# Four buffers for the second one-hots of the gate stage, made by VectorE and ScalarE in turn

## The chip, the cores and the metric

One Trainium2 chip, one core of it. The metric is the device time of one launch in microseconds (us), the median of three runs. PE is TensorE (PEld its weight loads), DVE VectorE, ACT ScalarE, POOL GpSimd, SP SyncE.

## What is computed

The kernel is a two-layer encoder over 256 positions of width 1024. The part of a layer that matters here is PEER, a retrieval of single-neuron experts with product keys:

```python
t1, i1 = lax.top_k(s1, PEER_TOPK)          # 16 of 128 first keys, per head
t2, i2 = lax.top_k(s2, PEER_TOPK)          # 16 of 128 second keys
top_s, top_c = lax.top_k(cand, PEER_TOPK)  # 16 of their 256 sums
experts = e1 * PEER_KEYS + e2
gates = jax.nn.softmax(top_s, axis=-1)
...
act = jax.nn.gelu(jnp.einsum('td,ted->te', h_c, expert_u[e_c]))
out = jnp.einsum('te,ted->td', g_c * act, expert_v[e_c])
```

A position has 8 heads with 16 experts each, so 128 (e1, e2) pairs with a gate each.

## The kernel before

The kernel doesn't gather experts. It runs all 16384 of them in 128 chunks ("up": h times a chunk of expert_u, then gelu; "down": the gated result times the chunk of expert_v) and weights them with a dense matrix `gates` that lives in the tile `arena`. The gate stage, between the up chunks and the down chunks of each layer, turns the 128 pairs of every position into that matrix. For one position it is a 128x128 product: the first one-hots (128 slots by 128 keys, each row scaled by its gate) with the second one-hots. Four positions (HOT = 4) make a batch, and there are 64 batches (N_BATCH) in a layer, written out without a loop. Batch t goes through these steps:

- DVE `hot_firsts`, on even batches only: the first one-hots of two batches at once, a comparison of 128x1024 into `v_raw` (four buffers, reused every four batches; with t the even batch of the pair, it waits until batch t-3 has been multiplied).
- POOL: one multiplication of 128x512 a batch, which scales the first one-hots by the gates (`s_gated`).
- `hot_second`: the second one-hots of the batch, 128x512, in one of three buffers. The first two are the tiles `w_hl` and DVE makes them in one comparison (t % 3 is 0 or 1). The third is the tile `act_w` and ACT makes it (t % 3 is 2) with four Square activations of 128x128 into `apart` (line 1214), a drain and one Relu of 128x512 (line 1216), all at once. Both wait until batch t-3 has been multiplied.
- PE: four fp32 matmuls of 128x128 (line 913; eight in the trace, as each takes two passes), into one of three PSUM banks. They wait for the copy of batch t-3 (`s_gates`), for `s_gated` and for `s_hot2`.
- DVE `gate_early`: the product of the bank and the first 48 chunks' gelu, 128x192, in place in `arena`.
- ACT: a copy of the other 80 chunks' columns, 128x320 (line 1228), after `gate_early` of the same batch.

Every engine takes its own work in the written order. DVE's order at step t is `hot_firsts(t+2)` if t is even, `hot_second(t+2)` if it is DVE's, `gate_early(t)`. ACT's is `hot_second(t+3)` if t % 3 is 2, then the copy of t. PE has five up chunks written in, after batches 7, 17, 27, 37 and 47 (`up_ahead`, line 811, 24 matmuls each). The high parts of the operands of four up chunks are made by ACT at t = 1, 5, 13 and 23 (`high_ahead`, line 1124) and their low parts by DVE after `gate_early` of t = 2, 6, 14 and 24 (`low_ahead`, a subtraction of 128x1024). DVE and POOL call most of their operations in helpers, so DVE's have line 1310 and POOL's line 1800; they are told apart by tile and shape: `v_raw<-ps,side` 128x1024 is `hot_firsts`, `w_hl<-ps,side` is DVE's `hot_second`, `arena<-arena,ps` 128x192 is `gate_early`, `u_hl` or `v_hl<-u_raw` 128x1024 is `low_ahead`, and on POOL `v_raw<-v_raw,side` is the scaling.

After batch 63 the down chunks begin: ACT's `high_v` and DVE's `low_v` of chunk 0 stand behind the stage's last copy.

Of the kernel before, what the change touches and what calls it, by code (L numbers as in the profile page):

```python
# [19 lines left out]
F32 = mybir.dt.float32  # L20
# [6 lines left out]
P = 128  # L27
D = 1024
S = 256
# [10 lines left out]
PK = 128  # L40
# [16 lines left out]
HOT = 4  # L57
# [16 lines left out]
def encoder(nc, x, w_in, w_out, w_glu, w_query, keys, expert_u, expert_v, rel_bias, gains,  # L74
            norm_final, ssm_par, ssm_b, ssm_c, consts, bucket_rows, out):
    ctx = ExitStack()
    with ctx:
# [3 lines left out]
        def sem(name):  # L81
# [30 lines left out]
        hot1_pair = [v_raw[i].rearrange("p (j n) -> p j n", j=2 * HOT) for i in range(2)]  # L112
        hot2 = [rows.rearrange("p r t -> p (r t)").rearrange("p (j n) -> p j n", j=HOT)
                for rows in (w_hl[0][:, :, :], w_hl[1][:, :, :], act_w[:, :, :])]
        early_hl = [u_hl[0][:, :, :, :], u_hl[1][:, :, :, :]] + [
            v_hl[i][:, :, :].rearrange("p r (k n) -> p r k n", k=DC) for i in range(2)]
        iota_ps_cols = slice(S, S + PK)
# [438 lines left out]
        def _(pe):  # L556
# [20 lines left out]
            with pe.Fori(0, DEPTH) as l:  # L577
# [325 lines left out]
                for t in range(N_BATCH):  # L903
                    b, batch = t % BATCHES, l * N_BATCH + t

                    pe.wait_ge(s_gates, batch + 2)
                    pe.wait_ge(s_gated, batch + 1)
                    if t % 3 < 2:
                        pe.wait_ge(s_hot2[0], l * (N_BATCH - N_BATCH // 3) + t // 3 * 2 + t % 3 + 1)
                    else:  # L910
                        pe.wait_ge(s_hot2[1], l * (N_BATCH // 3) + t // 3 + 1)
                    for j in range(HOT):
                        m = pe.matmul(ps[:, t % GATE_BANKS, j * P:(j + 1) * P], hot2[t % 3][:, j, :].bitcast(F32),  # L913
                                      hot1[b][:, j, :], start=True, stop=True)
                    m.then_inc(s_hot_free, 1)
                    if t % GAP_AHEAD == GAP_AHEAD - 3 and ahead < AHEAD:

                        if ahead == 4:
                            pe.wait_ge(s_gelu, 2 + l * PK + EARLY)
                        up_ahead(EARLY + ahead, ahead, early_hl[ahead % 4])  # L920
                        ahead += 1
# [28 lines left out]
        def _(act):  # L950
# [39 lines left out]
            with act.Fori(0, DEPTH) as l:  # L990
# [213 lines left out]
                act.activation(sel_T[:, 2, :], ps[:, 3, 0:S], ACT.Copy).then_inc(s_selT, 1)  # L1204

                split = {1: 4, 5: 5, 13: 6, 23: 7}
                def hot_second(t):

                    act.wait_ge(s_hot_free, l * N_BATCH + t + 2)
                    if t > 2:  # L1210
                        act.wait_ge(s_hot2[1], l * (N_BATCH // 3) + t // 3)
                    for j in range(HOT):
                        o = t * HOT + j
                        act.activation(apart[:, j, :], iota, ACT.Square, scale=-1.0, bias=sel_T[:, 1, o:o + 1])
                    act.drain()
                    act.activation(hot2[t % 3], apart[:, :, :], ACT.Relu, scale=-1.0, bias=one_c)\
                        .then_inc(s_hot2[1], 1)

                act.drain()
                hot_second(2)  # L1220
                for t in range(N_BATCH):
                    if t % 3 == 2 and t + 3 < N_BATCH:
                        hot_second(t + 3)
                    if t in split:
                        high_ahead(split[t])

# [60 lines left out]
        def _(dve):  # L1287
# [21 lines left out]
            def tt(o, a, b, op):  # L1309
                return dve.tensor_tensor(o, a, b, op)  # L1310
# [96 lines left out]
            with dve.Fori(0, DEPTH) as l:  # L1407
# [257 lines left out]

                def hot_second(t):

                    if t % 3 < 2:
                        dve.wait_ge(s_hot_free, l * N_BATCH + t + 2)
                        tt(hot2[t % 3], ps[:, 3, iota_ps_cols].unsqueeze(1).broadcast_to([P, HOT, PK]),  # L1670
                           sel_T[:, 1, t * HOT:(t + 1) * HOT].unsqueeze(2).broadcast_to([P, HOT, PK]),
                           ALU.is_equal).then_inc(s_hot2[0], 1)

# [284 lines left out]
```

## Time and profile before

| | |
|---|---|
| median of three runs | 2128.16 us (2127.49 to 2131.69) |
| the profiled execution's own time | 2125.18 us |
| its span, first to last instruction | 2123.4 us |
| gate stage, each of the two layers | 99.8 us (397.6 to 497.4 and 1445.4 to 1545.2) |
| PE, DVE, ACT, POOL busy over the span | 95%, 76%, 47%, 33% |
| mean granted TensorE clock | 0.988 of 2.4 GHz |

The profile is one execution; the time that is compared is the median. Busy shares of the whole span mix stages with different limits, so the gate stage is read by itself. An instruction's duration in a row includes its latency; two that follow each other at once on an engine start closer together than that, so the pitch (from start to start) is what an engine pays.

### The profile page before, as it was taken

The numbers are of one execution on the slowest core, as the hardware profiler recorded it, in microseconds if no ns is written. First come the engines' busy times: TensorE is split into PE (matmuls) and PEld (weight loads), VectorE is DVE, ScalarE is ACT, GpSimd is POOL, SyncE is SP. The second block draws the span as 40 slices with busy tenths as digits, with TensorE's granted clock in tenths as the row PEclk, the third lists the DMA queues.
The fourth block names the chain that finished last, engine by engine and source line by source line (L and its number), as shares of the span: only waits on it lengthen the run. The fifth ranks groups of instructions, "written<-read, shape, count | busy, mean of one in ns | idle before, by whom it ended". The sixth has DMA issues, their size and how long they took to land.

```text
span 2123.4 us, 37109 instructions
## 1 busy us (share of the span) xinstructions
PE 2022.9 (95%) x11526; PEld 1679.6 (79%) x11526; DVE 1605.3 (76%) x3087; ACT 989.7 (47%) x1627; POOL 695.9 (33%) x537
## 2 busy tenths in 40 slices
PE   7998999988999999999989999998899999999997
PEld 5764999887887888888867559998778788888886
DVE  6993676887779977777779738778867788777775
ACT  3543454664345444444444435546643544444443
POOL 6992566762000400000059816666600013000000
PEclk9999999999999999999999999999999999999999
DMA  5223454203558555555423235542055665555553
GB/s 195 90 71 144 171 183 160 86 21 119 192 198 292 182 196 187 188 188 187 139 91 102 98 134 189 165 146 71 11 170 195 205 219 182 188 188 190 187 192 112
DMA packets 90971, 330.41 MB, mean 156 GB/s; under 512 B 10452, under 2 KB 14676, under 8 KB 88573
## 3 DMA queue, kind: packets, MB, share of 16 engines
q1 hardware_dynamic: 90860, 329.23, 45.8%
q8 instruction: 48, 0.79, 0.1%
q14 instruction: 47, 0.38, 0.1%
q10 hardware_dynamic: 16, 0.02, 0.0%
HBM read 326.04 MB, written 3.16 MB: 155 GB/s over the span
## 4 chain that ended last, share of the span: by engine, by line
PE 78%; issue 7%; DVE 6%; POOL 4%; DVEq 2%; DMA 1%; ACT 1%; ACTq 0%; SPq 0%; POOLq 0%
PE ps L848 31%; PE ps L811 14%; PE ps L821 12%; PE ps L825 5%; PE ps L609 3%; POOL v_raw L1800 3%; PE ps L858 3%; PE ps L775 3%; DVE arena L1310 2%; PE ps L644 2%; PE ps L626 1%; PE ps L604 1%; DVE arena L1480 1%; DVEq L1730 1%; PE ps L727 1%
## 5 line engine op out<-in xcount | busy, mean ns | idle before, releaser
L848 PE MATMUL ps<-v_hl,w_hl 128*128 128x512 f32 x3072 | 734.2, 393 | 15.4 <-DVE v_hl L1310 15.3
L848 PEld LDWEIGHTS ps<-v_hl,w_hl 128*128 128x128 f32 x3072 | 577.4, 189 | 143.8 <-DVE v_hl L1310 22.5
L821 PE MATMUL ps<-h_hl,u_hl 128*128 128x512 f32 x1152 | 418.3, 397 | 0.0
L1800 POOL TENSOR_TENSOR arena<-arena 128x256 f32<-128x256 f32 (+1 forms) x225 | 213.8, 987 | 371.4 <-DVE arena L1310 368.6
L1310 DVE TENSOR_TENSOR v_hl<-v_raw,v_hl 128x1024 fp32r<-128x1024 f32 x208 | 258.6, 1243 | 49.3 <-ACT v_hl L1143 49.2
L825 PE MATMUL ps<-h_hl,u_hl 128*128 128x256 f32 x1008 | 282.6, 280 | 0.0
L1310 DVE TENSOR_TENSOR u_hl<-u_raw,u_hl 128x1024 fp32r<-128x1024 f32 x148 | 186.6, 1261 | 116.0 <-ACT u_hl L1105 113.7
L1143 ACT ACTIVATE v_hl<-v_raw 128x1024 fp32r<-128x1024 f32 x208 | 218.8, 1053 | 113.4 <-PE ps L848 98.9
L821 PEld LDWEIGHTS ps<-h_hl,u_hl 128*128 128x128 f32 x1152 | 216.4, 188 | 45.1
L1105 ACT ACTIVATE u_hl<-u_raw 128x1024 fp32r<-128x1024 f32 x144 | 152.3, 1058 | 135.3 <-PE ps L821 135.3
L1245 ACT ACTIVATE act_w<-act_w 128x256 f32<-128x256 f32 x144 | 60.2, 418 | 301.6 <-DVE act_w L1745 301.6
L825 PEld LDWEIGHTS ps<-h_hl,u_hl 128*128 128x128 f32 x1008 | 190.2, 189 | 5.6
L811 PE MATMUL ps<-h_hl,v_hl 128*128 128x256 f32 x1344 | 171.5, 285 | 0.2
L811 PE MATMUL ps<-h_hl,u_hl 128*128 128x256 f32 x1344 | 170.8, 285 | 0.0
L811 PEld LDWEIGHTS ps<-h_hl,v_hl 128*128 128x128 f32 x1344 | 164.8, 192 | 1.7 <-issue 0.6
L811 PEld LDWEIGHTS ps<-h_hl,u_hl 128*128 128x128 f32 x1344 | 164.6, 192 | 1.5
L1800 POOL TENSOR_TENSOR v_hl<-v_raw,v_hl 128x1024 fp32r<-128x1024 f32 x48 | 117.8, 2458 | 125.8 <-ACT v_hl L1116 125.7
L1800 POOL TENSOR_TENSOR v_raw<-v_raw,side 128x512 f32<-128x512 f32 x128 | 134.3, 1070 | 63.4 <-DVE v_raw L1310 63.4
L1800 POOL TENSOR_TENSOR u_hl<-u_raw,u_hl 128x1024 fp32r<-128x1024 f32 x52 | 125.3, 2417 | 77.1 <-ACT u_hl L1116 75.2
L1800 POOL TENSOR_TENSOR fence<-fence 128x1 f32<-128x1 f32 x3 | 2.7, 913 | 423.0 <-DVE w_hl L1310 407.0
L1310 DVE TENSOR_TENSOR arena<-ps,arena 128x512 f32<-128x512 f32 x164 | 101.9, 684 | 14.5 <-ACT arena L1091 5.0
L913 PE MATMUL ps<-v_raw,w_hl 128*128 128x128 f32 x688 | 93.2, 284 | 14.3 <-POOL v_raw L1800 8.1
(177 smaller groups left out, 2877.2 us busy)
## 6 DMA issues: line engine op xcount, KB each, us to landing
u_raw<-in_expert_u SPq DMA_DIRECT2D x208, 512.0 KB, 3.3
v_raw<-in_expert_v SPq DMA_DIRECT2D x208, 512.0 KB, 3.3
v_raw<-in_expert_u SPq DMA_DIRECT2D x48, 512.0 KB, 4.4
u_raw<-in_expert_v SPq DMA_DIRECT2D x48, 512.0 KB, 3.3
arena<-in_w_in SPq DMA_DIRECT2D x16, 512.0 KB, 3.8
arena<-in_w_in SPq DMA_DIRECT2D x8, 1024.0 KB, 5.1
arena<-in_ssm_b SPq DMA_DIRECT2D x16, 512.0 KB, 4.7
arena<-in_w_out SPq DMA_DIRECT2D x4, 2048.0 KB, 9.5
```

Of the source, the lines that this page charges most:

```text
L609: m = pe.matmul(ps[:, 1, o:o + S], w_slot[:, kind, k, :], hT[:, k, :], start=(k == 0), stop=(k == DC - 1))
L775: m = pe.matmul(ps[:, 4 + 2 * a + half, :], mixT[:, k, a * P:(a + 1) * P], w_out_sb[:, k, half * 512:(half + 1) * 512], start=(k == 0), st ...
L811: m = pe.matmul(ps[:, bank, o:o + S], hl[:, wp, k, :], h_hl[:, hp_, k, :], start=(k == 0 and j == 0), stop=(k == DC - 1 and j == 2))
L821: return pe.matmul(both, hl[:, 0, k, :], h_hl[:, :, k, :], start=(k == 0), stop=(k == DC - 1))
L825: pe.matmul(ps[:, bank, 0:S], hl[:, 1, k, :], h_hl[:, 0, k, :], start=False, stop=False)
L848: m = pe.matmul(ps[:, 2 * a + half, :], w_hl[s][:, wp, a * P:(a + 1) * P], v_hl[s][:, vp, half * 512:(half + 1) * 512], start=(first and j ...
L858: m = pe.matmul(ps[:, 6, 0:S], wq_slot[:, s, k, :], hT[:, k, :], start=(k == 0), stop=(k == DC - 1))
L913: m = pe.matmul(ps[:, t % GATE_BANKS, j * P:(j + 1) * P], hot2[t % 3][:, j, :].bitcast(F32), hot1[b][:, j, :], start=True, stop=True)
L1105: act.activation(u_hl[s][:, 0, :, :], u_raw[s][:, :, :], ACT.Copy).then_inc(s_u_hi, 1)
L1143: act.activation(v_hl[s][:, 0, :], raw, ACT.Copy).then_inc(s_v_hi, 1)
L1310: return dve.tensor_tensor(o, a, b, op)
L1800: return pool.tensor_tensor(o, a, b, op)
```

## The change

- A fourth buffer for the second one-hots, in unused columns of the tile `side`. Batch t uses buffer t % 4 (BATCHES is 4), and its maker waits for batch t-4 instead of t-3.
- DVE makes the second one-hots of the even batches, ACT those of the odd ones. Before, DVE made those with t % 3 of 0 or 1.
- ACT's work for a batch is in two functions. `hot_squares` (four Squares) stands before the copy of an odd batch t for batch t+4, `hot_second` (drain, wait, Relu) before the copy of an even batch t for batch t+3. Before, the wait and all six steps stood together.

```diff
+        hot2.append(side[:, 3 * S:3 * S + HOT * PK].rearrange("p (j n) -> p j n", j=HOT))
...
-                    if t % 3 < 2:
-                        pe.wait_ge(s_hot2[0], l * (N_BATCH - N_BATCH // 3) + t // 3 * 2 + t % 3 + 1)
-                    else:
-                        pe.wait_ge(s_hot2[1], l * (N_BATCH // 3) + t // 3 + 1)
+                    pe.wait_ge(s_hot2[t % 2], l * (N_BATCH // 2) + t // 2 + 1)
                     for j in range(HOT):
-                        m = pe.matmul(ps[:, t % GATE_BANKS, j * P:(j + 1) * P], hot2[t % 3][:, j, :].bitcast(F32),
+                        m = pe.matmul(ps[:, t % GATE_BANKS, j * P:(j + 1) * P], hot2[t % BATCHES][:, j, :].bitcast(F32),
                                       hot1[b][:, j, :], start=True, stop=True)
...
-                def hot_second(t):
-
-                    act.wait_ge(s_hot_free, l * N_BATCH + t + 2)
-                    if t > 2:
-                        act.wait_ge(s_hot2[1], l * (N_BATCH // 3) + t // 3)
+                def hot_squares(t):
+
+                    if t > 1:
+                        act.wait_ge(s_hot2[1], l * (N_BATCH // 2) + t // 2)
                     for j in range(HOT):
                         o = t * HOT + j
                         act.activation(apart[:, j, :], iota, ACT.Square, scale=-1.0, bias=sel_T[:, 1, o:o + 1])
+
+                def hot_second(t):
+
                     act.drain()
-                    act.activation(hot2[t % 3], apart[:, :, :], ACT.Relu, scale=-1.0, bias=one_c)\
+                    act.wait_ge(s_hot_free, l * N_BATCH + t + 1)
+                    act.activation(hot2[t % BATCHES], apart[:, :, :], ACT.Relu, scale=-1.0, bias=one_c)\
                         .then_inc(s_hot2[1], 1)
 
                 act.drain()
-                hot_second(2)
+                hot_squares(1)
+                hot_second(1)
+                hot_squares(3)
                 for t in range(N_BATCH):
-                    if t % 3 == 2 and t + 3 < N_BATCH:
+                    if t % 2 == 0 and t + 3 < N_BATCH:
                         hot_second(t + 3)
+                    if t % 2 and t + 4 < N_BATCH:
+                        hot_squares(t + 4)
                     if t in split:
                         high_ahead(split[t])
...
-                    if t % 3 < 2:
-                        dve.wait_ge(s_hot_free, l * N_BATCH + t + 2)
-                        tt(hot2[t % 3], ps[:, 3, iota_ps_cols].unsqueeze(1).broadcast_to([P, HOT, PK]),
+                    if t % 2 == 0:
+                        dve.wait_ge(s_hot_free, l * N_BATCH + t + 1)
+                        tt(hot2[t % BATCHES], ps[:, 3, iota_ps_cols].unsqueeze(1).broadcast_to([P, HOT, PK]),
```

## Rows read from the trace of the kernel before

**Rows 1.** The gate stages: busy us of PE, PEld, DVE, ACT, POOL; clock, DMA.

```profile
397.60:497.40 99.80, 82.63 (x646) 76.33 (x644) 86.35 (x144) 68.59 (x174) 67.17 (x64) 1.00 0.08 27
1445.40:1545.20 99.80, 82.80 (x646) 76.43 (x644) 86.32 (x143) 68.60 (x173) 67.17 (x64) 1.00 0.08 27
```

**Rows 2.** Group of one line in 398:500: busy us, mean ns, idle before.

```profile
L1310 DVE TENSOR_TENSOR w_hl<-ps,side 128x512 fp32r<-128x512 f32 x43 | 29.2, 681 | 0.0
```

**Rows 3.** Timeline of a stretch without an up chunk: start us, us, instruction, count.

```profile
483.89 1.22 DVE L1310 TENSOR_TENSOR v_raw<-ps,side 128x1024 f32<-128x1024 f32 x1
...
485.19 2.04 POOL L1800 TENSOR_TENSOR v_raw<-v_raw,side 128x512 f32<-128x512 f32 x2 [0.82 <-DVE v_raw L1310]
...
487.47 2.41 PE L913 MATMUL ps<-v_raw,w_hl 128*128 128x128 f32 x16
...
488.66 0.35 DVE L1310 TENSOR_TENSOR arena<-arena,ps 128x192 f32<-128x192 f32 x1 [0.43 <-PE ps L913]
488.93 1.22 DVE L1310 TENSOR_TENSOR v_raw<-ps,side 128x1024 f32<-128x1024 f32 x1
...
490.06 0.68 DVE L1310 TENSOR_TENSOR w_hl<-ps,side 128x512 fp32r<-128x512 f32 x1
...
491.78 1.22 DVE L1310 TENSOR_TENSOR v_raw<-ps,side 128x1024 f32<-128x1024 f32 x1
```

**Rows 4.** Timeline of ACT through one of its second one-hots.

```profile
442.78 0.44 ACT L1228 ACTIVATE arena<-ps 128x320 f32<-128x320 f32 x1 [1.92 <-DVE arena L1310]
443.12 1.27 ACT L1214 ACTIVATE apart<-cst,side 128x128 f32<-128x128 f32 x4
444.45 0.73 ACT L1216 ACTIVATE act_w<-apart,tiny 128x512 f32<-128x512 f32 x1
445.08 0.74 ACT L1228 ACTIVATE arena<-ps 128x320 f32<-128x320 f32 x2
```

**Rows 5.** Timeline of PE: the five up chunks inside the stage.

```profile
410.79 3.11 PE L811 MATMUL ps<-h_hl,v_hl 128*128 128x256 f32 x24
427.15 3.12 PE L811 MATMUL ps<-h_hl,u_hl 128*128 128x256 f32 x24
443.46 3.12 PE L811 MATMUL ps<-h_hl,u_hl 128*128 128x256 f32 x24
458.18 3.12 PE L811 MATMUL ps<-h_hl,v_hl 128*128 128x256 f32 x24
473.57 3.11 PE L811 MATMUL ps<-h_hl,v_hl 128*128 128x256 f32 x24
```

**Rows 6.** Timeline around the second up chunk.

```profile
426.24 1.15 PE L913 MATMUL ps<-v_raw,act_w 128*128 128x128 f32 x8 [0.83 <-POOL v_raw L1800]
...
431.20 0.35 DVE L1310 TENSOR_TENSOR arena<-arena,ps 128x192 f32<-128x192 f32 x1 [1.84 <-PE ps L913]
...
431.58 0.44 ACT L1228 ACTIVATE arena<-ps 128x320 f32<-128x320 f32 x1 [1.47 <-DVE arena L1310]
...
432.36 1.22 DVE L1310 TENSOR_TENSOR v_raw<-ps,side 128x1024 f32<-128x1024 f32 x1
```

**Rows 7.** Timeline where low parts and POOL meet, and where ACT is late.

```profile
411.75 1.79 DVE L1310 TENSOR_TENSOR u_hl<-u_raw,u_hl 128x1024 fp32r<-128x1024 f32 x1 [1.15 <-ACT u_hl L1124]
...
422.98 3.02 POOL L1800 TENSOR_TENSOR v_raw<-v_raw,side 128x512 f32<-128x512 f32 x2 [0.22 <-DVE v_raw L1310]
...
423.69 1.42 DVE L1310 TENSOR_TENSOR v_hl<-u_raw,v_hl 128x1024 fp32r<-128x1024 f32 x1
...
440.25 1.64 DVE L1310 TENSOR_TENSOR v_hl<-u_raw,v_hl 128x1024 fp32r<-128x1024 f32 x1 [1.30 <-ACT v_hl L1124]
...
470.14 1.28 ACT L1214 ACTIVATE apart<-cst,side 128x128 f32<-128x128 f32 x4 [0.99 <-PE ps L913]
```

**Rows 8.** Timeline at the stage's end: the last copy, then the next stage.

```profile
496.93 0.44 ACT L1228 ACTIVATE arena<-ps 128x320 f32<-128x320 f32 x1 [0.56 <-DVE arena L1310]
497.39 0.29 DVE L1718 TENSOR_SCALAR w_hl<-arena 128x256 fp32r x1 [0.49 <-issue]
```

## The prediction

> **What bounds the kernel now.** I read the page first, then the stage's busy times, its groups by line, and the timeline. The change touches the gate stage alone, 99.8 us in each layer. In it no engine is full: DVE is busy 86.35 us by its records, PE 82.63, ACT 68.59, POOL 67.17, at a granted clock of 1.00 [rows 1]. Where no engine is full, a loop through several of them sets the time, so I looked for the loop in the timeline. Between the up chunks it is this [rows 3]. The first one-hots of batches 56 and 57 start on DVE at 483.89. POOL starts 1.30 us later and takes 1.02 for each of the two batches. The matmuls of batch 57 start 0.24 after POOL's second (487.23; in the record from 487.47 they are the first eight), gate_early(57) starts at 488.66, and behind it are the first one-hots of 60, at 488.93, which reuse the buffer. That is 5.04 us for four batches: the POOL loop. The next pair starts at 491.78, 2.85 later, by DVE's own pitch: first one-hots 1.13 (to 490.06), then twice a second one-hot and a gate_early, 1.72 together. A gate_early alone has a pitch of 0.27 (488.66 to 488.93), so a second one-hot has 0.59 (0.86 less 0.27). Of each three pairs one has two of DVE's second one-hots, the others one (1.13 + 0.59 + 0.54 = 2.26). Six batches take 5.04 + 2.85 = 7.89 us, 1.315 a batch.
>
> An up chunk adds a stall. Call T the end of the last matmul ahead of it (PE starts the up chunk some 0.24 before that). For the second, T is 427.39; gate_early of the next batch is at T + 3.81, its copy at T + 4.19, the next first one-hots that must wait at T + 4.97 [rows 6]. The up chunks start 16.36, 16.31, 14.72 and 15.39 us apart [rows 5]. The POOL loop alone gives 4.97 + 5.04 + 4.73 (the last loop counts only to the end of its second batch's matmuls: 1.30 + 2.04 + 0.24 + 1.15) = 14.74, and one interval shows 14.72: this is the floor. What lies above it, 0.65 in the last, 1.62 and 1.57 in the first two, is delay by others. In the last, ACT's Squares for batch 47 waited for batch 44 until 470.14 [rows 7]. In the first two it is the low parts: they wait 1.15 and 1.30 us for ACT's high part, behind its second one-hot, and where one starts ahead of POOL's second batch, POOL's pair takes 3.02 us instead of 2.04 [rows 3, 7].
>
> **The change part by part.** *DVE* makes 32 second one-hots a layer instead of 43 [rows 2]: 11 x 0.59 = 6.5 us less a layer, 13.0 in both. This is the ceiling of the gain and not the gain, since every pair now costs 2.26 us, under the POOL loop's 2.52: the detour of 2.85 is gone, but the POOL loop stays.
>
> *ACT* makes 32 instead of 21 (a third of 64). Its pitches [rows 4]: a copy followed by a Square 0.34; the four Squares 1.27 to 1.28 to the last one's end, so 0.30 each from start to start (one lasts about 0.39), 1.20 for all four with something other than a drain behind them; Squares to Relu over the drain 1.33, which leaves about 0.07 for the drain; Relu to copy 0.63. New is a copy ahead of the drain: 0.44 + 0.07 = 0.51. Two batches now take ACT 1.20 + 0.51 + 0.63 + 0.34 = 2.68 us. From above, with nothing overlapped, the durations give 1.28 + 0.44 + 0.07 + 0.73 + 0.44 = 2.96. I take 2.68, because each part of it but the 0.51 is a pitch seen; 2.96 stays for the range. 2.68 is longer than the loop's 2.52, so ACT is slower than POOL between up chunks. But it needn't make up a whole up stall: the copy behind the stall starts at T + 4.19, and the matmuls of the tenth batch need the copy six batches on: 4.19 + 3 x 2.68 + 0.44 + 0.13 + 1.15 = 13.95 us. A high part in the interval adds 0.97, so 14.9. Both are below the POOL path.
>
> *Buffers and split.* ACT's Squares wait for no matmul any more, only for its own Relu two odd batches back, which is long done. A Relu waits for batch t-4, whose matmuls precede a copy that ACT has made already. So the wait of batch 47 goes: 0.6 us. In PE's queue nothing new is waited for.
>
> *Low parts.* High part 5 now has only four Squares ahead of it, not Squares and Relu. That is 0.63 us earlier (411.1 for the low part that started at 411.75 [rows 7]), so the first one-hots behind it don't hold up batch 10. For the low part after batch 14: ACT's copy of 12 is at T + 4.19 + 5.36 = 9.55, then 0.34 + 1.20 + 1.04 + 0.04, so it starts at T + 12.17. POOL's scaling of batch 16 runs until 4.97 + 5.04 + 1.30 + 1.02 = T + 12.33. The low part is there first, by 0.16 us, and POOL pays the 0.98 as it did at 422.98. The interval is 10.01 + 1.30 + 3.02 + 0.24 + 1.15 = 15.72. The one with batch 24 is built alike.
>
> The rows show an exclusion: 1.42, 1.64 and 1.79 us for one subtraction of the same shape, longer the more of a POOL operation is left when it starts, and POOL's pair longer by 0.98 when it waits instead [rows 7]. The Trainium skill says so on the page "SBUF — State Buffer", section "Who interferes with whom": a DVE instruction with two SBUF inputs and a GpSimd one that reads SBUF lock each other out for the whole instruction. The trace agrees. By that rule, should the low part come after POOL's start, POOL would lose nothing and DVE would wait; the interval would then be 14.9 by ACT's path, which I price as a rival.
>
> *The sum for a layer,* before against after: until the first up chunk nothing (POOL's loop sets it); intervals 16.36 to 15.72 is 0.64; 16.31 to 15.72 is 0.59; 14.72 to 14.72 is 0; 15.39 to 14.74 is 0.65. The tail: from T = 473.57 + 0.25 = 473.82 (the second up chunk starts 0.24 before its T) to the end of the last copy at 497.37 [rows 8] is 23.55. After: the copy of 60 is at 4.19 + 6 x 2.68 = 20.27, then 0.44 + 0.13 + 1.15 for it and the matmuls of 63, 0.06 + 0.38 for gate_early, 0.44 for the copy, so 22.9: 0.65. Together 2.53 us a layer, 5.1 for both. The next stage begins directly behind the last copy [rows 8], and the second layer's stage is as long and as busy as the first's [rows 1], so all of it should reach the end. The profiled execution, 2125.18 us with a span of 2123.4, would take about 2120.1; it is 2.98 below the median, and the median goes from 2128.16 to 2123.1. A difference under 0.2% (4.3 us) is about what a measurement of this kernel can't tell from no change.
>
> **The rivals.** *More gain: the low parts miss POOL.* If ACT is later than worked out by 0.16 us at T + 12.17, POOL's second batch starts ahead of the low part. Both intervals drop from 15.72 to about 14.9, 3.3 us in both layers, and the time is about 2119.8. For it: the margin is two ACT rounds wide, 0.08 each, and the new wait behind the drain may cost some hundredths. Against: every term but one is a pitch seen.
>
> *Little: ACT overlaps nothing.* At 2.96 a round the paths are 4.19 + 8.88 + 1.72 = 14.8, with a high part 15.85, and the tail 4.19 + 17.76 + 2.6 = 24.55. Against before: 0.51 + 0.46 - 0.08 + 0.59 - 1.0 = 0.5 a layer, so 2127.2, no change that can be told. For it: 723 ns of Relu and 0.44 of copy are now interleaved with drains; against: Relu to copy is 0.63 in the rows.
>
> *Slower: ACT becomes the bound.* Each 0.1 above 2.96 costs 0.3 in each of four intervals and 0.6 in the tail, 1.8 a layer. The gain is gone at 2.99, and from 3.12 on the kernel is slower by more than 0.2%; at 3.2 it would be about 2136. That takes a further exposed latency of 0.4 in each round of 2.68; the drain behind a copy, which no row shows, is the only place for it. The Trainium skill has a rule against the change, on "ScalarE: Activation LUTs", section "Rules for kernel authors": relu, add and the like belong on VectorE and not on ScalarE. The rows agree on the price, a pitch of 1.33 + 0.63 on ACT against 0.59 on DVE [rows 3, 4], but the rule doesn't say whether the engine had room, and ACT has 31 of 99.8 us idle [rows 1]. What it stands for is this rival.
>
> **How the numbers follow.** Forecast 0.40 (gain 3 to 7, most of it over 4.3), low parts miss POOL 0.30, little 0.18, slower 0.12 (half of it by more than 0.2%, and then some more for unseen causes, so 0.11). Faster by over 0.2%: 0.27 + 0.29 = 0.56. Within: 0.13 + 0.01 + 0.18 + 0.01 = 0.33. Slower: 0.11. The range is 2117.5 to 2128.5: below, the bigger gain with 2 us of error; above, the case of little gain and 1.5 of error. The slower case is left out, and under 0.1 of the others.
>
> **What would show it.** Up chunks 15.7, 15.7, 14.7 and 14.8 us apart, the stage at about 97.3 us; DVE's second one-hots 32 a layer, pairs of first one-hots never 2.85 apart by DVE's pitch; POOL still 3.02 for the pair at batch 16. Relu starting 0.51 behind an odd copy confirms ACT's round; 0.6 or more refutes it. PE waiting mostly for ACT's copies would mean the rival of an ACT bound. It would be wrong altogether if the next stage started no earlier.

## The result and the profile after

The changed kernel takes 2117.07 us (median of four runs, 2114.93 to 2118.31) against 2129.93 us (2127.49 to 2133.59): ratio 0.9937, 95% interval 0.9919 to 0.9956. Measured again it is 0.9944 (0.9931 to 0.9957). So it is faster, by 9 to 17 us by the first interval and 9 to 15 by the second, where 5.1 were forecast and 2117.5 was the lower end of the range. The two profiled executions differ by 10.3 us (2125.18 and 2114.93).

The stage first, as in [rows 1]: busy us of PE, PEld, DVE, ACT, POOL, then clock and DMA, from the first Square to the last copy of each layer.

```profile
400.00:495.20 95.20, 80.11 (x646) 75.02 (x644) 81.91 (x132) 86.33 (x228) 66.13 (x64) 1.00 0.08 28
1440.80:1536.10 95.30, 80.19 (x647) 75.11 (x645) 81.65 (x132) 86.45 (x228) 66.14 (x64) 1.00 0.08 29
```

From the first Square's start to the last copy's end the stage is 95.26 us long (399.96 to 495.22), 4.54 less in a layer and 9.1 in both. ACT went from 68.6 to 86.3 us busy and is now the busiest engine; DVE went from 86.3 to 81.9. The groups by line of the same stretch, which answer to [rows 2]:

```profile
L1805 POOL TENSOR_TENSOR v_raw<-v_raw,side 128x512 f32<-128x512 f32 x64 | 66.1, 1055 | 28.1 <-DVE v_raw L1315 28.1
L1211 ACT ACTIVATE apart<-cst,side 128x128 f32<-128x128 f32 x128 | 40.6, 390 | 0.1
L1217 ACT ACTIVATE side<-apart,tiny 128x512 f32<-128x512 f32 x16 | 11.6, 723 | 2.6 <-PE ps L911 0.4
...
L1315 DVE TENSOR_TENSOR w_hl<-ps,side 128x512 fp32r<-128x512 f32 x16 | 10.9, 678 | 0.0
L1315 DVE TENSOR_TENSOR act_w<-ps,side 128x512 f32<-128x512 f32 x16 | 10.8, 678 | 0.0
```

DVE makes the second one-hots of 32 batches (16 in each of its two tiles), and ACT's 128 Squares are those of the other 32, as the code says. The up chunks, which answer to [rows 5]:

```profile
412.94 3.11 PE L812 MATMUL ps<-h_hl,v_hl 128*128 128x256 f32 x24
427.95 3.12 PE L812 MATMUL ps<-h_hl,u_hl 128*128 128x256 f32 x24
442.99 3.12 PE L812 MATMUL ps<-h_hl,u_hl 128*128 128x256 f32 x24
457.50 3.11 PE L812 MATMUL ps<-h_hl,v_hl 128*128 128x256 f32 x24
472.00 3.11 PE L812 MATMUL ps<-h_hl,v_hl 128*128 128x256 f32 x24
```

| us | to the first up chunk | four intervals | last up chunk to last copy | stage |
|---|---|---|---|---|
| before | 13.22 | 16.36, 16.31, 14.72, 15.39 | 23.80 | 99.80 |
| forecast | 13.22 | 15.72, 15.72, 14.72, 14.74 | 23.15 | 97.3 |
| after | 12.98 | 15.01, 15.04, 14.51, 14.50 | 23.22 | 95.26 |

The tail (from the last up chunk to the last copy) was right. Two things were not: the intervals with a low part are 0.7 shorter than forecast, and the floor of 14.73 is 14.51. Here are the high part, POOL's pair and the low part of the first interval, which answer to [rows 7], and PE's next matmuls:

```profile
424.43 1.04 ACT L1122 ACTIVATE v_hl<-u_raw 128x1024 fp32r<-128x1024 f32 x1
424.46 2.04 POOL L1805 TENSOR_TENSOR v_raw<-v_raw,side 128x512 f32<-128x512 f32 x2 [0.73 <-DVE v_raw L1315]
...
425.51 2.07 DVE L1315 TENSOR_TENSOR v_hl<-u_raw,v_hl 128x1024 fp32r<-128x1024 f32 x1 [0.27 <-ACT v_hl L1122]
...
425.93 2.27 PE L911 MATMUL ps<-v_raw,w_hl 128*128 128x128 f32 x16 [0.91 <-ACT arena L1233]
```

POOL's pair is two operations. The second has its own record:

```profile
425.45 1.04 POOL L1805 TENSOR_TENSOR v_raw<-v_raw,side 128x512 f32<-128x512 f32 x1
```

It starts at 425.45 and the low part at 425.51, 0.06 us later. So it is DVE's low part that waits: it takes 2.07 us, where the same subtraction with no POOL operation beside it takes 1.22 (e11). POOL's pair takes its 2.04. The forecast had them 0.16 apart the other way round. In the second interval the low part starts at 440.54, 0.15 us behind POOL's second batch, and takes 1.97. The matmuls of batch 16 then wait 0.91 us for ACT's copy of batch 13, so this interval ends on ACT's path and no longer on POOL's.

ACT's round, two batches long, in the tail (the columns are those of [rows 4]):

```profile
484.06 0.72 ACT L1217 ACTIVATE w_hl<-apart,tiny 128x512 fp32r<-128x512 f32 x1
...
484.69 0.41 ACT L1233 ACTIVATE arena<-ps 128x320 f32<-128x320 f32 x1
...
485.01 1.27 ACT L1211 ACTIVATE apart<-cst,side 128x128 f32<-128x128 f32 x4
...
486.18 0.42 ACT L1233 ACTIVATE arena<-ps 128x320 f32<-128x320 f32 x1
...
486.75 0.72 ACT L1217 ACTIVATE side<-apart,tiny 128x512 f32<-128x512 f32 x1
```

It is 2.69 us (0.63, 0.32, 1.17, 0.57), where 2.68 was worked out. The copy ahead of the drain, which no row of before showed, costs 0.57 and not 0.51; the other three terms together are 0.05 shorter than taken.

### The profile page after: what moved, and what is told of

Its sections match the earlier page's. It is cut to its first block, busy times and chain, and to the rows that moved or that the text cites. A ratio compares the mean times of both kernels' runs of the same rounds, so it can differ in the third digit from the quotient of the medians.

```text
span 2113.1 us, 37179 instructions
## 1 busy us (share of the span) xinstructions
PE 2013.9 (95%) x11526; PEld 1675.6 (79%) x11526; DVE 1594.4 (75%) x3065; ACT 1025.4 (49%) x1737; POOL 694.4 (33%) x537
## 4 chain that ended last, share of the span: by engine, by line
PE 75%; POOL 7%; issue 7%; DVE 5%; DVEq 2%; ACT 2%; DMA 1%; POOLq 1%; ACTq 0%; SPq 0%
PE ps L849 31%; PE ps L812 14%; PE ps L822 12%; PE ps L826 5%; PE ps L859 3%; POOL arena L1805 3%; POOL v_raw L1805 3%; PE ps L776 3%; PE ps L610 2%; DVE arena L1315 2%; POOL u_raw L1805 1%; PE ps L645 1%; PE ps L728 1%; DVE arena L1485 1%; PE ps L605 1%
## 5 line engine op out<-in xcount | busy, mean ns | idle before, releaser
L849 PE MATMUL ps<-v_hl,w_hl 128*128 128x512 f32 x3072 | 731.6, 392 | 14.7 <-DVE v_hl L1315 14.6
L1141 ACT ACTIVATE v_hl<-v_raw 128x1024 fp32r<-128x1024 f32 x208 | 218.9, 1053 | 112.1 <-PE ps L849 96.6
L1750 DVE TENSOR_REDUCE act_w<-ps 128x256 f32<-128x512 f32 x144 | 98.3, 683 | 0.8 <-PE ps L822 0.8
```

The lines of the kernel that those rows point to most:

```text
L849: m = pe.matmul(ps[:, 2 * a + half, :], w_hl[s][:, wp, a * P:(a + 1) * P], v_hl[s][:, vp, half * 512:(half + 1) * 512], start=(first and j ...
L1141: act.activation(v_hl[s][:, 0, :], raw, ACT.Copy).then_inc(s_v_hi, 1)
L1750: dve.tensor_reduce(act_w[:, s, :], ps[:, bank, :].rearrange("p (r t) -> p t r", r=2), AX.X, ALU.add) .then_inc(s_pre_late, 1)
```

## The experiments

The runs carry the labels of their headings below. "To first up" runs from the first Square to the first up chunk, the intervals are the distances from one up chunk to the next. Stage and intervals are those of layer 0; "both layers" is what the two stages gain against before. The stages of the two layers agree within 0.21 us.

| run | to first up | intervals | tail | stage | both layers | ratio (95% interval) |
|---|---|---|---|---|---|---|
| after_again | 12.98 | 15.01, 15.02, 14.51, 14.51 | 23.22 | 95.25 | 8.9 | 0.9944 (0.9931 to 0.9957) |
| e1 | 13.16 | 16.41, 16.30, 14.72, 14.92 | 23.79 | 99.30 | 1.0 | 0.9996 (0.9986 to 1.0006) |
| e2 | 12.98 | 15.44, 15.54, 14.51, 14.60 | 23.53 | 96.60 | 6.3 | 0.9971 (0.9959 to 0.9983) |
| e3 | 12.98 | 15.04, 15.05, 14.52, 14.60 | 23.26 | 95.45 | 8.7 | 0.9945 (0.9928 to 0.9962) |
| e4 | 12.97 | 15.44, 15.54, 14.51, 14.59 | 23.53 | 96.58 | 6.3 | 0.9973 (0.9961 to 0.9986) |
| e10 | 15.26 | 16.48, 16.25, 15.28, 15.30 | 24.44 | 103.01 | -6.4 | 1.0026 (1.0014 to 1.0037) |
| e5 | 12.97 | 15.44, 15.48, 14.51, 14.60 | 23.23 | 96.23 | 7.1 | 0.9951 (0.9934 to 0.9967) |
| e6 | 13.12 | 15.45, 15.44, 14.50, 14.60 | 22.90 | 96.01 | 7.5 | 0.9955 (0.9939 to 0.9972) |
| e8 | 11.89 | 14.51, 14.51, 14.56, 14.60 | 23.22 | 93.29 | 13.0 | 0.9910 (0.9893 to 0.9928) |
| e16 (e8 again) | 11.91 | 14.67, 14.51, 14.60, 14.60 | 23.23 | 93.52 | 12.8 | 0.9922 (0.9906 to 0.9937) |
| e13 | 11.89 | 14.51, 14.61, 14.61, 14.61 | 23.52 | 93.75 | 12.2 | 0.9932 (0.9918 to 0.9946) |
| e9 | 11.90 | 16.33, 14.80, 14.73, 15.38 | 23.81 | 96.95 | 5.7 | 0.9959 (0.9944 to 0.9973) |
| e11 | 11.90 | 14.36, 14.35, 14.35, 14.08 | 23.23 | 92.27 | 15.1 | 0.9913 (0.9896 to 0.9930) |
| e12 | 11.98 | 14.73, 14.74, 14.72, 14.73 | 23.12 | 94.02 | 11.6 | 0.9924 (0.9911 to 0.9937) |
| e14 | 11.97 | 14.62, 14.56, 14.61, 14.60 | 23.22 | 93.58 | 12.7 | 0.9939 (0.9918 to 0.9960) |
| e17 | 11.97 | 14.73, 14.72, 14.73, 14.73 | 23.30 | 94.18 | 11.2 | 0.9930 (0.9910 to 0.9950) |
| e15 | 11.91 | 14.52, 14.67, 14.52, 14.61 | 22.90 | 93.13 | 13.5 | 0.9930 (0.9917 to 0.9944) |
| e18 | 14.24 | 17.27, 17.25, 17.53, 16.31 | 27.20 | 109.80 | about -20 | 1.0087 (1.0069 to 1.0104) |

One interval can differ between layers and executions of the same kernel: in e8 and e16 the eight lie between 14.51 and 14.67, and the last two of after_again are 14.60 and 14.61 in the second layer. So a difference of 0.1 in a single interval shows nothing.

**after_again, the changed kernel once more.** No edit.

> The changed kernel once more, as the measure for the rest. Its gate stage took 95.3 us a layer against 99.8 before, 9.1 us in both, while the medians differ by 12.9. If the stage is all of the gain, the ratio here is about 0.9957 (9.1 of 2128), and the stage is again 95.3 us. If something outside the stage changed as well, the ratio stays at 0.994 or below with the same stage.

The stage is the same to 0.01 us. The ratio lies between the two expectations, and its interval just holds 0.9957. More on this below.

**e1, the fourth buffer alone,** on the kernel before. The lines show ACT's part; the same edit stands at DVE's and PE's places.

```diff
-        act.wait_ge(s_hot_free, l * N_BATCH + t + 2)
+        act.wait_ge(s_hot_free, l * N_BATCH + t + 1)
...
-        act.activation(hot2[t % 3], ...)
+        act.activation(hot2[t % BATCHES], ...)
```

> The kernel before with four buffers for the second one-hots, DVE still making two of three. Theory (DVE's share sets it): only ACT's wait for batch 44 ahead of 47 goes, 0.65 us a layer, and a little at the low parts, so the stage takes 98.5 to 99.2 us and the kernel gains 1 to 2.5 us. Rival (the fourth buffer is what helped): the stage falls to about 95.5 us.

99.3 us, just above the range expected: the last interval falls from 15.39 to 14.92, nothing else moves by more than 0.06. The buffer alone is not what helps.

**e2, no split,** on the changed kernel: Squares and Relu of batch t+3 together, ahead of the copy of the even batch t.

```diff
-                    if t % 2 and t + 4 < N_BATCH:
-                        hot_squares(t + 4)
...
+                        hot_squares(t + 3)
                         hot_second(t + 3)
```

> The changed kernel with ACT's Squares and Relu for a batch together again, ahead of the copy of the even batch. Theory (the POOL loop bounds, ACT has little slack): ACT's round is 2.60 us, but a copy stands behind 1.96 us of work, which puts the path from an up chunk to the tenth batch at 14.55 us against 14.50 of the POOL loop, and 15.5 with a high part; the stage takes 96 to 97 us. Rival (the split is what pays): above 98.5 us.

96.6 us, as expected, but the reason was another than I wrote. The intervals without a low part are the same within 0.1 us, so a copy behind 1.96 us of ACT work costs nothing there. In those with one, the timeline shows POOL's pair at 3.02 and the low part ahead of its second batch:

```profile
425.83 3.02 POOL L1803 TENSOR_TENSOR v_raw<-v_raw,side 128x512 f32<-128x512 f32 x2 [0.63 <-DVE v_raw L1313]
...
426.53 1.42 DVE L1313 TENSOR_TENSOR v_hl<-u_raw,v_hl 128x1024 fp32r<-128x1024 f32 x1
```

**e3, three buffers,** on the changed kernel (`t % 3`, waits for batch t-3).

> The changed kernel with three buffers (t % 3), each maker waiting for batch t-3. Theory: a Relu behind an up chunk now comes after the stall, 0.26 us on ACT's path, which counts in the two intervals with a high part and in the tail; the stage takes 95.5 to 96.3 us. Rival (the fourth buffer carries the gain): 98 us or more.

95.45 us, 0.2 more. The second layer's stage of after_again is 95.45 us as well, so the fourth buffer is worth 0.2 us a layer at most.

**e4, only who makes what:** e2 and e3 together.

> Only who makes what is changed: DVE the even batches, ACT the odd ones, with three buffers and ACT's work in one piece that waits for the matmuls of t. Theory: both ACT savings are needed together, because after an up chunk the whole 1.96 us of Squares and Relu come after the stall and ahead of a copy; the intervals are about 15.5 and 16.4 us, the tail 24.5, the stage 100 to 102 us, so no faster than before. Rival (the reassignment alone carries the gain, as the runs with three buffers and without the split suggest): below 97 us.

A miss: 96.6 us, the same as e2. The expectation had ACT's work in one piece behind the wait, but in this kernel the Squares stand ahead of the wait, which holds back only the Relu. In the kernel before the wait comes first; e10 does that.

**e10, the wait first:** as e4, with ACT's wait for batch t moved ahead of the Squares.

```diff
                 def hot_squares(t):
+                    act.wait_ge(s_hot_free, l * N_BATCH + t + 2)
```

> DVE the even, ACT the odd batches, three buffers, and ACT waits for the matmuls of batch t ahead of the Squares for t+3, as the kernel before does. Theory (Squares ahead of the wait are what the change needs, not the fourth buffer nor the Relu apart): after an up chunk 1.96 us of ACT work lie between the matmuls and the copy; intervals 15.3 and 16.2 us, tail 24.3, stage 99.5 to 101 us, no faster than before. Rival: 96.6 us as with the Squares ahead of the wait.

103.0 us, and the kernel is slower than before, by a ratio of 1.0026. The mechanism is the one expected, the stretch to the first up chunk (15.26) was not worked out and is the rest. Part of that stretch is the clock: its mean is 0.91 there in both layers and 1.00 in the rest of the stage, and the sixteen matmuls that start at 410.67 take 3.50 us, where sixteen take 2.05 in the changed kernel. The timeline behind an up chunk:

```profile
434.37 0.35 DVE L1314 TENSOR_TENSOR arena<-arena,ps 128x192 f32<-128x192 f32 x1 [1.68 <-PE ps L911]
434.44 1.28 ACT L1212 ACTIVATE apart<-cst,side 128x128 f32<-128x128 f32 x4 [2.16 <-PE ps L911]
...
435.79 0.72 ACT L1218 ACTIVATE w_hl<-apart,tiny 128x512 fp32r<-128x512 f32 x1
436.42 0.74 ACT L1232 ACTIVATE arena<-ps 128x320 f32<-128x320 f32 x2
```

gate_early is done at 434.72, but ACT idles 2.16 us, then makes the one-hots, and its copy starts at 436.42. With the Squares ahead of the wait the same copy starts 0.4 us behind gate_early's start. So the reassignment pays only because the Squares no longer stand behind the wait. Nothing else differs in the code of e4, and its stage is 6.4 us a layer shorter, about 1.5 of which is the lower clock in e10's first stretch (3.50 less 2.05).

**e5, the high parts earlier,** on the changed kernel.

```diff
-                split = {1: 4, 5: 5, 13: 6, 23: 7}
+                split = {1: 4, 5: 5, 12: 6, 22: 7}
```

> The changed kernel with ACT's high parts 6 and 7 one step earlier (before the copies of 12 and 22); DVE's low parts stay where they are. In the changed kernel the low part starts 0.03 us after POOL's second batch and POOL loses nothing. Theory (the order of arrival is what made the intervals 15.0 us and not 15.7): the low part is now ready about 0.4 us ahead of POOL's second batch, POOL's pair takes 3.0 us, the two intervals are about 15.7 us and the stage about 96.6. Rival (the intervals are ACT's path, and POOL's blocking is hidden): 15.0 us or less, stage 95.3 or less.

The two intervals grow from 15.01 and 15.04 to 15.44 and 15.48 and the stage to 96.2. The timeline shows the order turned round, low part ahead of POOL's second batch, whose own record starts at 422.97 (and the 0.03 us of the expectation is 0.06 by the records of the changed kernel):

```profile
421.97 3.02 POOL L1805 TENSOR_TENSOR v_raw<-v_raw,side 128x512 f32<-128x512 f32 x2 [0.63 <-DVE v_raw L1315]
...
422.67 1.42 DVE L1315 TENSOR_TENSOR v_hl<-u_raw,v_hl 128x1024 fp32r<-128x1024 f32 x1
```

**e6, half of ACT's Squares left out.**

```diff
-                    for j in range(HOT):
+                    for j in range(HOT if t < 4 else 2):
```

> The changed kernel with two of ACT's four Squares per batch left out from batch 5 on (two positions of each odd batch then carry old one-hots). ACT's round falls from 2.68 to 2.08 us. Theory (outside the intervals with low parts the POOL loop bounds, and ACT's lateness is what lets the low parts miss POOL): intervals without low parts stay at 14.5, those with low parts grow from 15.0 to about 15.7, the tail falls by 0.3; the stage is about 96.2 us, longer with less work. Rival (ACT bounds): the stage falls by 2 us or more.

96.0 us: 0.75 more than with all Squares, though the tail is 0.3 less. With less work ACT hands over the high part sooner, and POOL is blocked again (its pair is 3.02 us in both intervals). The output of this kernel is wrong, since two positions of each odd batch keep old one-hots; only its times are used.

**e8, the parts moved into the stalls,** on the changed kernel.

```diff
-                split = {1: 4, 5: 5, 13: 6, 23: 7}
+                split = {1: 4, 8: 5, 18: 6, 28: 7}
...
-                low_after = {2: 4, 6: 5, 14: 6, 24: 7}
+                low_after = {7: 4, 17: 5, 27: 6, 37: 7}
```

> The changed kernel with the high parts 5, 6, 7 on ACT before the copies of 8, 18, 28 and the low parts 4 to 7 on DVE after gate_early of 7, 17, 27, 37, where both engines wait for an up chunk. Theory: a high part costs ACT 0.97 of an idle 1.1 us, a low part delays nothing that is due before T + 4.97, and POOL is not blocked on the path; all four intervals become 14.5, the first stretch 12.0, the tail stays 23.2, the stage takes 93.2 to 93.6 us. Rival (the low part then delays the first one-hots of the stall and so the matmuls behind it): intervals of 15 us or more.

93.3 us, as expected, with intervals up to 0.1 above the 14.5. The low part lies in the up chunk's stall:

```profile
425.08 3.11 PE L812 MATMUL ps<-h_hl,u_hl 128*128 128x256 f32 x24
...
425.64 1.77 DVE L1315 TENSOR_TENSOR u_hl<-u_raw,u_hl 128x1024 fp32r<-128x1024 f32 x1
...
427.33 1.21 DVE L1315 TENSOR_TENSOR v_raw<-ps,side 128x1024 f32<-128x1024 f32 x1
...
428.62 2.04 POOL L1805 TENSOR_TENSOR v_raw<-v_raw,side 128x512 f32<-128x512 f32 x2 [2.29 <-DVE v_raw L1315]
...
430.29 1.22 DVE L1315 TENSOR_TENSOR v_raw<-ps,side 128x1024 f32<-128x1024 f32 x1
```

With T = 425.32 (the end of the last matmul ahead of the up chunk, as in the prediction), the first one-hots that must wait start at T + 4.97, where [rows 6] has them. By its median this is the fastest kernel here that does all of the work. The same kernel once more is e16:

> The kernel with the parts moved into the stalls, once more. Its stage is 6.5 us a layer shorter than before, 13.0 in both, so the ratio should be 0.9939. Its first measurement was 0.991. If it is 0.991 to 0.992 again, 4 to 6 us of the difference lie outside the stage; if it is near 0.994, they were scatter.

**e9, the same move on the kernel before.**

> The kernel before, with nothing of the change, but the high and low parts moved as in the run before this one (high parts before the copies of 8, 18, 28, low parts after gate_early of 7, 17, 27, 37). Theory (low parts and POOL are one cost, DVE's detours and ACT's waits another): the first stretch falls to 12.2, the first two intervals from 16.3 to 14.7 to 15.0, the last stays at 15.4 and the tail at 23.8; the stage takes 95.5 to 96.5 us. Rival (moving pays only where DVE has the smaller share): 98 us or more.

96.95 us, 0.45 above the expected range, because the first interval stayed at 16.33: there a second one-hot of ACT, which waits for the first batch behind the up chunk, comes ahead of the moved high part, and the copies behind both. The move is worth 2.8 us a layer by itself; reassigning adds 3.7 on top of it (96.95 to 93.29), and 4.5 without it.

**e13, the parts moved, no split.**

> The kernel with the parts moved into the stalls and ACT's Squares and Relu together again. Without the split the intervals with parts were 15.45 us and POOL's pair took 3.02. Theory (the split mattered through the order of arrival of low part and POOL alone): with the parts away all intervals are 14.5 to 14.6 and only the tail is 0.3 longer, the stage takes 93.6 us. Rival (a copy behind 1.96 us of ACT work costs by itself): intervals with a high part of 14.9 us or more, stage 94.3 or more.

93.75 us. Without low parts on POOL's way the split is worth the 0.3 of the tail and some hundredths an interval.

**e11, half of POOL's scaling left out,** on e8: two of the four positions of each batch keep gate 1, so the output is wrong.

> The kernel with the parts moved into the stalls, and POOL scaling only two of the four positions of each batch (the other two keep gate 1). Theory (the POOL loop sets the 14.5 us): the intervals fall until ACT's path binds, 13.95 us, the tail stays at 23.2 because ACT sets it already, the stage takes 90.8 to 91.3 us against 93.3. Rival (ACT or DVE sets the 14.5): no change, 93 us or more.

92.3 us, half of the fall expected. POOL's pair takes 1.19 us instead of 2.04, and the intervals fall by 0.15 to 0.5, so the POOL loop was the bound of this kernel's intervals; but the next path is 0.15 below it and not 0.6. The last interval, whose stretch has only a low part in the stall, is 14.08; the 13.95 of the forecast left out that a part in a stall pushes the first copy back.

**e12, the last batch on DVE,** on e8. The lines show PE's waits; the makers and their own waits are changed to match.

```diff
-                    pe.wait_ge(s_hot2[t % 2], l * (N_BATCH // 2) + t // 2 + 1)
+                    if t % 2 and t < N_BATCH - 1:
+                        pe.wait_ge(s_hot2[1], l * (N_BATCH // 2 - 1) + t // 2 + 1)
+                    else:
+                        pe.wait_ge(s_hot2[0], l * (N_BATCH // 2 + 1) + (t + 1) // 2 + 1)
```

> The kernel with the parts moved into the stalls, and the second one-hots of the last batch, 63, made by DVE (33 on DVE, 31 on ACT). Theory (the tail is ACT's path, the rest is not): the tail falls from 23.2 to 22.9, where the POOL loop holds it, everything else stays; the stage takes 93.0 us. Rival (DVE has no room): the tail grows by DVE's 0.6 us.

A miss that led on: the tail is down only 0.1, and every interval is 14.73, though nothing in them was changed but the numbers PE waits for. In the kernel before, the two batches of a pair waited for different numbers too.

**e14 and e17, the numbers alone,** on e8.

> The kernel with the parts moved into the stalls; the semaphore for DVE's second one-hots starts at 7 and PE waits for values higher by 7 in the even batches. Nothing else differs. In that kernel the even and the odd batch of a pair wait for the same number, and the trace has 62 register operations of PE's sequencer for it instead of 124. Theory (with the same number the second batch of a pair starts 0.1 us earlier, and that sits on the POOL loop twice an interval): intervals 14.73 instead of 14.51, first stretch 12.0, stage 94.0 to 94.3 us. Rival (the floor fell for another reason): 93.3.

```diff
-                    pe.wait_ge(s_hot2[t % 2], l * (N_BATCH // 2) + t // 2 + 1)
+                    pe.wait_ge(s_hot2[t % 2], l * (N_BATCH // 2) + t // 2 + (1 if t % 2 else 51))
...
+            for _ in range(2):
+                dve.sem_inc(s_hot2[0], 25)
```

(That is e17, where DVE's semaphore starts 50 higher and PE waits for 50 more; e14 has 7 for the 50.)

> As the run with the other wait values, but the semaphore starts at 50, so no number of an even batch is that of any odd batch of the layer. Theory: the trace has about 124 register operations at PE's wait for the second one-hots, all four intervals are 14.7 and the first stretch 12.0, the stage takes 93.9 to 94.1 us. Rival: 93.4, and the floor fell for a reason that stays open.

e14 tells little: 76 register operations instead of 62, the first stretch 0.08 longer and the rest nearly as it was. e17 has all four intervals at 14.72 to 14.73 and the stage at 94.2. Here are the register operations of PE's sequencer at the wait for the second one-hots (count, duration in ns). The kernel before has two lines for it, 124 operations together; then come the changed kernel and e17:

```profile
L909 PEldq ALU_OP  x84: 32/32/32, 401.1 to 1543.1; - x84
L911 PEldq ALU_OP  x40: 32/32/32, 407.1 to 1542.1; - x40
```

```profile
L909 PEldq ALU_OP  x62: 32/32/32, 404.6 to 1532.9; - x62
```

```profile
L909 PEldq ALU_OP  x126: 32/32/32, 401.7 to 1530.8; - x126
```

Where nothing else holds PE back, the groups of the two batches of a pair start 0.89 us apart with equal numbers and 0.99 with different ones; the weight loads, first of e8, then of e17:

```profile
483.80 0.97 PEld L911 LDWEIGHTS ps<-v_raw,act_w 128*128 128x128 f32 x8 [0.49 <-issue]
...
484.69 0.97 PEld L911 LDWEIGHTS ps<-v_raw,side 128*128 128x128 f32 x8
```

```profile
483.98 0.97 PEld L911 LDWEIGHTS ps<-v_raw,act_w 128*128 128x128 f32 x8 [0.29 <-issue]
484.97 0.97 PEld L911 LDWEIGHTS ps<-v_raw,side 128*128 128x128 f32 x8
```

**e15, the last batch on DVE with the numbers kept** (it counts on `s_hot2[1]`). The lines show its new place in DVE's order.

```diff
...
+                    if t == N_BATCH - 3:
+                        hot_second(N_BATCH - 1)
```

> The kernel with the parts moved into the stalls, DVE makes the second one-hots of batch 63 (after gate_early of 61, and counts them on ACT's semaphore, so PE's waits keep their numbers). Theory: intervals 14.5 as without it, tail 22.9 to 23.0 instead of 23.2, stage 93.0 us. If the intervals are 14.73 again, the numbers were not the cause.

93.1 us with a tail of 22.90, the shortest stage with all of the work in it. Its median is 2112.0 against 2109.5 for e16 on the same chip, so the 0.7 us that its two stages are shorter can't be seen in the time.

**e18, six Squares for four,** on e8 (two more, into unused columns).

> The kernel with the parts moved into the stalls, and two more Squares of 128x128 in each of ACT's second one-hots (into unused columns). ACT's round is 3.28 instead of 2.68 us. By the prediction's formula for ACT's path (4.19 and three rounds and 1.72, 0.3 more with a low part in the stall) the intervals are 15.8 to 16.1, the tail 26.8, the first stretch about 13.2, the stage 103 to 104 us, so the kernel is about 8 us slower than before. If ACT had slack to hide the 0.6, the stage stays below 96.

109.8 us and a ratio of 1.0087: worse than the 103 to 104 expected. ACT's round in the trace is 3.26 us, as worked out, and the tail (27.20) is 0.4 above what was expected. The first stretch is 1.0 longer than worked out, and the intervals with a high part are 0.9 to 1.2 longer than the one without: ACT is busy 104.0 of the 109.8 us and has no idle time left that would hide a high part, even in the stall. So ACT as the bound is a real danger at this spot: 0.6 us more a round turns a gain of 13 us into a loss of about 20.

## Why the prediction was wrong

**What bounds.** Right for the intervals without a low part. There the loop of DVE's first one-hots, POOL and PE is the bound after the change: halving POOL's work shortens every interval once the parts are out of the way (e11), and leaving ACT work out shortens neither of the two (e6). For the kernel before no such experiment was made; there the loop rests on the rows. In the two intervals with a low part ACT's path is the bound after the change, as the rival below has it. That 6.5 us a layer off DVE is only the ceiling held as well.

**ACT.** Right in its size: round 2.69 for 2.68, tail 23.22 for 23.15, and the rival in which ACT makes the kernel slower did not come about. The Trainium skill's rule on "ScalarE: Activation LUTs", section "Rules for kernel authors", that adds and relus belong on VectorE would have spoken for a loss. The result says otherwise here, and e18 shows how near the loss is.

**The low parts.** This is the step that failed: "The low part is there first, by 0.16 us, and POOL pays the 0.98". It came 0.06 us after the start of POOL's second batch (0.15 in the other interval), so the rival with a chance of 0.30 took place, "the low parts miss POOL", priced at 14.9 an interval and 2119.8 us; measured 15.01 and 15.04. In the first interval the low part came at T + 12.33 and not T + 12.17. Nearly all of that is the first copy behind the up chunk, which is at T + 4.34 and not T + 4.19: low part 5 held up DVE and so gate_early. POOL's second batch came at T + 12.27 and not T + 12.33: the loop was shorter, and POOL's two operations start 1.00 apart and not 1.02. The rows of before already had both cases: the low part at 423.69 took 1.42 us and blocked POOL, but the one at 440.25 took 1.64 and had missed it, and the sum let both intervals pay. e5 and e6 confirm the cause, since both make ACT earlier and both lengthen the intervals, with POOL's pair at 3.02 us. But a blocked interval is 15.45 and not the 15.72 of the sum, so the price of the step was too high as well: in e5 the loop ahead of it is 0.11 shorter (T + 9.90 for T + 10.01), and PE starts 0.11 behind POOL's pair and not 0.24. Together the step is 0.7 us in each of two intervals.

**The floor.** The step "this is the floor" failed too: 14.74 was built of loops of 5.04 us, and the change made the number that PE waits for the same in both batches of a pair. That takes a register operation away for each pair, starts the second batch 0.1 us sooner, and brings an interval to 14.51 (e17 puts it back to 14.73, and e12 did so unintended). It is worth 0.2 us in each interval and 0.08 in the stretch ahead of the first; the other 0.16 there I have not taken apart.

**Buffers and split.** The forecast gave both no price but the wait of batch 47. That was right for the buffer (0.5 us alone, 0.2 at most as part of the change). The split is worth 0.3 in the tail, and 0.4 to 0.5 in each interval with a low part through the order of arrival (e2). What it didn't see is that moving the Squares ahead of the wait is a condition of all the rest: with the wait first the same reassignment is a loss (e10), by more than the lower clock there explains.

**The sum.** For a layer 2.53 were forecast and 4.54 measured: 0.24 in the first stretch, 1.39 in the low parts' intervals, 0.45 in the others, less 0.07 in the tail.

**Outside the stage.** "The change touches the gate stage alone" put the rest at nothing. The two stages account for 9.1 us; the two ratios make it 13.4 (9.4 to 17.2) and 11.9 (9.2 to 14.7). With the 9.1 alone the median would have been about 2119, inside the range. A good part of the rest is visible in the profiles: the 12 us behind each stage, first two of before, then two of the changed kernel.

```profile
497.40:509.40 12.00, 9.64 (x31) 7.73 (x32) 6.51 (x12) 4.12 (x4) 0.00 (x0) 0.72 0.56 193
1545.20:1557.20 12.00, 9.61 (x31) 7.70 (x32) 6.50 (x12) 4.13 (x5) 0.00 (x0) 0.72 0.55 182
```

```profile
495.20:507.20 12.00, 9.59 (x35) 7.79 (x36) 7.53 (x12) 4.15 (x5) 0.00 (x0) 0.86 0.61 213
1536.10:1548.10 12.00, 9.61 (x35) 7.77 (x36) 7.50 (x12) 4.14 (x5) 0.00 (x0) 0.86 0.60 211
```

In both kernels TensorE is granted 1.2 GHz for a while behind the stage (0.51 of 2.4 GHz from 498 to 501 us in the changed kernel), but the mean granted clock of these stretches is 0.72 before and 0.86 after (0.86 in after_again too). Over all profiles, what follows the second stage takes 574.8 to 575.9 us where this clock is 1.00, 576.7 to 577.8 where it is 0.86, and 577.5 to 578.7 where it is 0.72. From before to after the two stretches behind the stages (to the second stage, to the end) are 3.6 us shorter together, and the stretch ahead of the first stage, where the code is the same, is 2.4 longer; that one scatters from 397.4 to 402.2 us over the profiles.

**What stays open.** Whether the change brings the higher clock about is not shown: it varies between executions of one kernel (0.72 and 1.00 behind the two stages of e8, 1.00 and 1.00 in e16). The executions of before have a mean clock of 0.988 (64 of them), ten of the changed kernel 0.990. For e1, e2, e4 and e10 the stage alone explains the ratio within 0.0004; for e8 and e16 it gives 0.9939 and 0.9940, and they measured 0.9910 and 0.9922, with intervals that end just below. So 3 to 6 us of the gain of the changed kernel, e8 and e16 lie outside the stage or in how the executions of before scatter (2122 to 2134 us in one set), and one profile of each kernel can't tell how much is which.

## What to carry to other kernels

Where no engine is full, add up the loops through several engines, each to its next start, and add up the next longest too: here it lay 0.15 to 0.5 us below the first, in an interval of 14.5 (e11). An operation that locks another engine out has a price that depends on which of the two comes first. When the sum puts them 0.16 us apart, as here, either can happen, and the forecast should sit between the two cases; better, put the operation where both engines wait (93.3 us here against 95.3). Put the part of an engine's work that needs no wait ahead of the wait (96.6 us in e4 against 103.0 in e10).

## What the runs showed of the hardware

Leaving out half of an engine's Squares made the stage longer, 96.0 us against 95.3, because a DVE subtraction with two SBUF inputs and POOL's multiplication do not run at the same time: POOL's pair took 3.02 us where the subtraction was there first (both such intervals of e2, e4, e5 and e6) and 2.04 where it was late, by 0.06 and 0.15 us in the changed kernel. The sequencer's register operations of 32 ns ahead of PE's waits are not free: one for each pair of batches, next to nothing in the busy times, moved a whole stage from 93.3 to 94.2 us (e8 and e17), as it sat on the loop that bounds. Behind the gate stage TensorE is granted 1.2 GHz for a stretch of different length in different executions, and with it goes the time of the rest of the kernel, 574.8 us behind the second stage at the shortest and 578.7 at the longest.
